# Attention scores of a MoBA and mLSTM block: three 64-row products per pair of heads, or two 128-row products per head with the split ahead of device memory

## The reference, cut to what matters

```python
h = rms_norm(x, pre_norm_g[l])
proj = jnp.einsum('bsd,dc->bsc', h, w_in[l])
aq, ak, av, az, mq, mk, mv, mo, mz, mi, mf = split_columns(proj)
ya = moba_attention(partial_rope(att_heads(aq), pos), partial_rope(att_heads(ak), pos), att_heads(av))
ya = rms_norm(ya, attn_out_g[l]) * jax.nn.silu(az)
...
s_own = jnp.einsum('hqd,hld->hql', q_c, k_own).astype(jnp.float32)
p = jax.nn.softmax(jnp.concatenate([s_sel, s_own], axis=-1), axis=-1)
...
y = jnp.einsum('bsc,cd->bsd', jnp.concatenate([ya, ym], axis=-1), w_out[l])
x = x + rms_norm(y, post_norm_g[l])
```

## Time and profile before

| what | value |
|---|---|
| median of 3 runs | 317.83 us (317.74 to 318.38) |
| the profiled execution | 317.99 us, its span 316.2 us |
| PE busy | 309.4 us, 98% of the span, granted clock 0.998 |
| DVE busy | 225.4 us, 71% |
| ACT busy | 165.2 us, 52% |
| POOL busy | 95.9 us, 30% |
| DMA | 38.30 MB, mean 121 GB/s |
| score products (L1758) | 96 of 64 rows by 128 |

### The profile page before, as it was taken

How to read it: one execution, slowest core, us unless ns; L and a number is a source line. 1 busy time by engine, 2 the same in 40 slices (tenths; PEclk the granted TensorE clock), 3 DMA queues, 4 the chain that set the end, 5 groups by cost and what they waited for, 6 DMA issues and landing times.

```text
span 316.2 us, 4992 instructions
## 1 busy us (share of the span) xinstructions
PE 309.4 (98%) x1599; PEld 256.4 (81%) x1599; DVE 225.4 (71%) x508; ACT 165.2 (52%) x336; POOL 95.9 (30%) x118
## 2 busy tenths in 40 slices
PE   8999999999999999999999999999999999999992
PEld 4888888888888888888888888778888888888882
DVE  2544999748998699968998568964577766856534
ACT  3548857287345324663157563384556876353301
POOL 8201006056350213002320025592711984000000
PEclk9999999999999999999999999999999999999999
DMA  7941553956725486645864332210220473310111
GB/s 222 323 99 38 153 149 93 170 163 150 134 68 146 134 158 205 188 124 122 180 227 151 102 90 77 73 66 31 67 68 0 125 200 145 133 68 0 68 66 67
DMA packets 29081, 38.30 MB, mean 121 GB/s; under 512 B 3624, under 2 KB 15184, under 8 KB 29056
## 3 DMA queue, kind: packets, MB, share of 16 engines
q1 hardware_dynamic: 27424, 34.51, 36.2%
q0 software_dynamic: 1472, 3.34, 7.0%
q10 hardware_dynamic: 160, 0.14, 0.1%
HBM read 33.68 MB, written 4.29 MB: 120 GB/s over the span
## 4 chain that ended last, share of the span: by engine, by line
PE 93%; issue 3%; DMA 2%; DVE 0%; DVEq 0%; SPq 0%; ACT 0%; POOLq 0%; POOL 0%; ACTq 0%
PE bank L1476 24%; PE bank L1478 24%; PE bank L1477 24%; PE bank L1814 3%; PE bank L1524 3%; PE bank L1758 3%; PE bank L1779 3%; PE bank L1612 2%; DMA farena<-in_x 2%; PE bank L1708 1%; PE bank L1505 1%; PE bank L1769 1%; PE bank L1613 1%; PE bank L1552 1%; PE bank L1551 1%
## 5 line engine op out<-in xcount | busy, mean ns | idle before, releaser
L778 ACT ACTIVATE w_hi<-w_raw 128x512 fp32r<-128x512 f32 x71 | 43.7, 626 | 63.2 <-PE bank L1478 51.1
L1476 PE MATMUL bank<-w_hi,xT_hi 128*128 128x512 f32 (+1 forms) x180 | 72.5, 403 | 0.0
L1478 PE MATMUL bank<-w_hi,xT_lo 128*128 128x512 f32 (+1 forms) x180 | 69.8, 388 | 0.0
L1477 PE MATMUL bank<-w_lo,xT_hi 128*128 128x512 f32 (+1 forms) x180 | 69.3, 385 | 0.0
L1043 DVE TENSOR_TENSOR w_lo<-w_raw,w_hi 128x512 fp32r<-128x512 f32 x64 | 45.5, 721 | 11.1 <-ACT w_hi L778 11.0
L1476 PE MATMUL bank<-xT_hi,w_hi 128*128 128x512 f32 x128 | 50.8, 397 | 0.0
L1478 PE MATMUL bank<-xT_hi,w_lo 128*128 128x512 f32 x128 | 50.1, 392 | 0.0
L1477 PE MATMUL bank<-xT_lo,w_hi 128*128 128x512 f32 x128 | 50.0, 390 | 0.0
L1478 PEld LDWEIGHTS bank<-w_hi,xT_lo 128*128 128x128 f32 x180 | 33.8, 188 | 7.2
L1476 PEld LDWEIGHTS bank<-w_hi,xT_hi 128*128 128x128 f32 x180 | 33.9, 188 | 5.8 <-issue 0.4
L1477 PEld LDWEIGHTS bank<-w_lo,xT_hi 128*128 128x128 f32 x180 | 34.0, 189 | 5.5
(11 more groups left out here) (211 smaller groups left out, 581.8 us busy)
## 6 DMA issues: line engine op xcount, KB each, us to landing
w_raw<-in_w_in SPq DMA_DIRECT2D x72, 256.0 KB, 2.9
w_raw<-in_w_out SPq DMA_DIRECT2D x16, 256.0 KB, 2.7
kq_rows<-stage SPq DMA_DIRECT2D x8, 256.0 KB
gy<-kq_rows SPq DMA_DIRECT2D x8, 256.0 KB, 3.5
gy<-in_x SPq DMA_DIRECT2D x4, 512.0 KB, 5.4
out_y<-gy SPq DMA_DIRECT2D x7, 256.0 KB, 2.1
farena<-in_x SPq DMA_DIRECT2D x4, 256.0 KB, 5.3
farena<-in_x SPq DMA_DIRECT2D x2, 512.0 KB, 7.5
```

Of the source, the lines that this page charges most:

```text
L778: a.activation(hi, raw, ACT.Copy).then_inc(w_hi_done, 1)
L1476: pe.matmul(o, hi, m_hi, start=start, stop=False)
L1477: pe.matmul(o, hi, m_lo, start=False, stop=False)
L1478: return pe.matmul(o, lo, m_hi, start=False, stop=stop)
```

## The change

The split into high and low parts moves ahead of device memory, where ACT writes the high part to `gate` and DVE the low part over `stage`. Each quarter is written out twice, high and low. What comes back is, for each head, one operand of 128 partitions: 64 high rows over 64 low rows (`keys`, `queries`), and for the queries a second one with the two halves exchanged (`swapped`). A head's scores are then two products of all 128 rows, stacked queries by stacked keys and exchanged queries by stacked keys, which adds the low-by-low product to the three. The reads move from SP to POOL: 8 for keys, 8 for queries, and 10 for the exchanged queries.

```diff
-OUT_AT, BACK_AT = (S_AQ + 6, S_AV + 6), (S_AQ + 8, S_AV + 8)
+HIGH_AT, LOW_AT = (S_AQ + 1, S_AV + 1), (S_AQ + 2, S_AV + 2)
+OUT_AT = (S_AQ + 13, S_AV + 13)
+FIRST_Q = 3
...
-OUT_CUTS = {0: 5, 1: 6, 2: 7, 3: 8, 12: 17, 13: 17, 14: 19, 15: 20}
+OUT_CUTS = {0: 5, 1: 8, 2: 9, 3: 11, 12: 17, 13: 17, 14: 19, 15: 20}
...
             def rows_out(w, m):
-                sp.wait_ge(kq_ready, NT * w + m + 1)
-                sp.dma_start(kq_dram[w, :, ROT * m:ROT * m + ROT, :], by_dims[:, m, :]).then_inc(kq_out[w], 16)
-            def rows_back(w, m):
-                sp.wait_ge(kq_out[w], 16 * NT)
...
+                for q, (done, src) in enumerate(((kq_hi, gate), (kq_lo, by_dims))):
+                    sp.wait_ge(done, NT * w + m + 1)
+                    sp.dma_start(kq_dram[w, :, q, ROT * m:ROT * m + ROT, :], src[:, m, :]).then_inc(kq_out[w], 16)
...
+                    if OUT_AT[w] <= n < OUT_AT[w] + NT:
+                        rows_out(w, n - OUT_AT[w])
...
+            def keys_back(h):
+                g.wait_ge(kq_out[0], 32 * NT)
+                g.dma_start(keys[:, h, :], head_rows(0, h).bitcast(F32R)).then_inc(keys_in, 16)
+            def queries_back(h):
+                g.wait_ge(kq_out[1], 32 * NT)
...
+                g.dma_start(queries[:, h, :], head_rows(1, h).bitcast(F32R)).then_inc(queries_in[h >= FIRST_Q], 16)
...
             for h in range(1, MH):
+                if h == MH - 1:
+                    for n in range(AH):
+                        keys_back(n)
                 decay_rows(h)
...
+            swapped_back(3)
+            for h in range(FIRST_Q):
+                queries_back(h)
             for b in range(S_MZ + 2, LAST_SLOT + 1):
                 cut(b + AHEAD)
...
                 if b == S_MZ + 5:
                     head_rsqrt(2 * MH - 1)
+                    for h in range(FIRST_Q, AH):
+                        queries_back(h)
+                    swapped_back(2)
...
-            def k_high(m):
-                a.wait_ge(kq_moved[0], 16 * NT)
-                a.activation(kT_hi[:, m, :], whole[:, m, :], ACT.Copy).then_inc(kt_hi, 1)
+            def kq_high(w, m):
+                a.wait_ge(kq_ready, NT * w + m + 1)
+                if w:
+                    a.wait_ge(kq_out[0], 32 * NT)
+                a.activation(by_dims_hi[:, m, :], by_dims[:, m, :], ACT.Copy).then_inc(kq_hi, 1)
             def v_copy(t):
                 projected(a, "av", t)
-                a.wait_ge(kq_out[1], 16 * NT)
+                a.wait_ge(kq_out[1], 32 * NT)
...
                 if w and m == 0:
-                    v.wait_ge(kq_out[0], 16 * NT)
+                    v.wait_ge(kq_out[0], 32 * NT)
...
+            def kq_low(w, m):
+                v.wait_ge(kq_hi, NT * w + m + 1)
+                v.tensor_tensor(by_dims_lo[:, m, :], by_dims[:, m, :], f32(by_dims_hi[:, m, :]),
+                                ALU.subtract).then_inc(kq_lo, 1)
...
+                pe.matmul(o, queries[:, h, t * P:(t + 1) * P], k, start=True, stop=False)
+                pe.matmul(o, swapped[t][:, h // 2, h % 2, :], k, start=False, stop=True).then_inc(score_ps, 1)
```

More of the change, by code:

```diff
@@ L115 @@
 N_WIDE = AH * (NT - 1)
-FOURS_FROM = AH * (NT - 2)
 EVENTS = {}
@@ L312, in build @@
         bcol = pcol[0:16, R_BIAS:R_END]
-        by_dims, whole = stage, gate
+        by_dims, by_dims_hi = stage, gate.bitcast(F32R)
+        by_dims_lo = stage[:].bitcast(F32R)
         rope_t = [f_part(F_COS, SEQ), f_part(F_SIN, SEQ)]
@@ L448, in build @@
         kq_out = [sem(f"kq_out{w}") for w in range(2)]
-        kq_moved = [sem(f"kq_moved{w}") for w in range(2)]
+        kq_hi = sem("kq_hi")
+        kq_lo = sem("kq_lo")
+        keys_in = sem("keys_in")
+        queries_in = [sem(f"queries_in{c}") for c in range(2)]
+        swapped_in = [sem(f"swapped_in{t}") for t in range(NT)]
         v_raw = sem("v_raw")
-        kt_hi = sem("kt_hi")
-        kt_lo = sem("kt_lo")
         v_hi_done = sem("v_hi_done")
         v_lo_done = sem("v_lo_done")
-        qt_hi = sem("qt_hi")
-        qt_lo = sem("qt_lo")
         score_ps = sem("score_ps")
@@ L872, in v_high @@
                              ACT.Copy).then_inc(v_hi_done, 1)
-            def q_high(m):
-                a.wait_ge(kq_moved[1], 16 * NT)
-                a.wait_ge(mpv_ps, MH * NT)
-                a.activation(q_hi[:, m, :], whole[:, m, :], ACT.Copy).then_inc(qt_hi, 1)
             def turn_high(n):
@@ L922, in _ @@
                             v_high(t)
-                if S_AQ + 5 <= b < S_AQ + 5 + NT:
-                    k_high(b - S_AQ - 5)
-                if S_MZ + 5 <= b < S_MZ + 7:
-                    q_high(2 * (b - S_MZ - 5))
-                    q_high(2 * (b - S_MZ - 5) + 1)
+                for w in range(2):
+                    if HIGH_AT[w] <= b < HIGH_AT[w] + NT:
+                        kq_high(w, b - HIGH_AT[w])
             def out_cut(n):
@@ L1290, in _ @@
                             v_low(m)
-                if S_AQ + 6 <= b < S_AQ + 6 + NT:
-                    k_low(b - S_AQ - 6)
+                for w in range(2):
+                    if LOW_AT[w] <= b < LOW_AT[w] + NT:
+                        kq_low(w, b - LOW_AT[w])
                 if b - 2 in PE_PV and PE_PV[b - 2][1] % 2 == 1:
@@ L1796, in _ @@
                 events = EVENTS.get(s, ())
[L1797 to L1801 removed]
+                if s < NU:
+                    scores(s)
                 for kind, what in events:
```

126 lines of the change are left out of this document (60 added, 66 removed).

## The result

| | before | changed |
|---|---|---|
| median, us | 318.14 (317.74 to 318.57, 6 runs) | 330.87 (329.64 to 332.75, 6 runs) |
| profiled execution, us | 317.99 | 330.92 |
| its span, us | 316.2 | 329.1 |
| PE's slot 56 begins, us | 182.51 | 192.61 |
| PE's last product begins, us | 310.36 | 322.76 |

The changed kernel takes 1.040 of the time before (95% interval 1.037 to 1.044). The forecast of 321.4 has the sign and less than a third of the size, and the time lies outside the range of 315.9 to 323.8.

What follows compares the result with a forecast made beforehand. PE was taken as the bound, with 93% of the chain of waits. From 317.99 us, -2.1 for PE's scores and +5.5 for the writes gave 321.4 us, range 315.9 to 323.8.

Steps and rivals of the forecast that it cites:

- The place and the sign: Release of `stage` to `v_copy`, just before PE's slot 56, decides; 321.4 us, 1.1% slower.
- Half of them work: DMA engines during writes: busy 0.48 of the time at 186 GB/s, so 256 KB takes 1.4 us.
- Term 2: Writes of keys and queries from `stage`: late release starts slot 56 near 188.0, not 182.5; +5.5 us, bounds nothing to 7.
- The stall of head 3: PE waits for DVE's `qk_low` of head 3 after slot 52: 0.6 us, inside the 5.5, no own term.
- rival 2: PE's clock falls in the 4.9 us stall before slot 56, losing 1.7 us: 323.1 us; chance 0.15.
- Term 1: PE's attention scores: two 128-row products per head take 9.7 us in place of 11.8; -2.1 us, bounds 2.1 and 0.3.
- The signs: Trace marks listed beforehand to show each step right or wrong, such as PE idle 4 to 5.5 us near 183.
- The edits costed at nothing: Splits, moved `q_high` and `q_low`, POOL's reads, later decay rows and mask waits: no time added.

Runs made afterwards that it cites:

- sixteen in the slowest dimension: Changed kernel with scratch rows reordered so each write's slowest dimension is 16, not 8; 322.68 us, ratio 1.014 to the kernel before.
- keys alone with sixteen: Changed kernel with only the keys' rows written and read with slowest dimension 16, queries keeping 8; 326.17 us, ratio 1.024 to the kernel before.
- reads on SP: Changed kernel with the four exchanged reads of the last tile on SP in place of POOL; 330.61 us, ratio 1.036 to the kernel before.
- one slot earlier: Changed kernel with each pair of writes one slot earlier in SP's order; 328.39 us, ratio 1.033 to the kernel before.
- PE kept at work: Changed kernel with 24 unread products of 512 columns into an idle bank ahead of slot 56; 329.00 us, ratio 1.035 to the kernel before.
- loads cut: Changed kernel with weight loads of slots 60 to 65 cut to 16 of 512 columns; 325.14 us, ratio 1.023 to the kernel before.

## Why the prediction was wrong, step by step

- **The place and the sign were right.** PE stood still just before slot 56, ended by `v_copy` (L907), which waited for the writes, and DVE was held near 147. "Half of them work" was right too: sixteen in the slowest dimension took 8 us off.
- **Term 2, the length of a burst, is the step that failed.** "Eight writes with three loads between them take 8 x 1.4 + 3 x 0.7 = 13.3 us", with 1.4 more to land, gave 14.7; the bursts lasted 17.0 and 16.6 us. The two prices were right (the write's came from a single stretch of 1 us in the earlier trace rows, which was lucky): 1.35 us a write with the loads' bytes away, and 11.5 to 12.0 us from the first landing to the last, where the sum had 11.9. What was too small is the start. The first write was to land 2.8 us after its issue and took 4.8 and 4.9. Some 0.9 of that went with the loads' bytes, so it belongs to the loads that already stood in front, which the sum took as none. The other 1.3 us stayed (4.1 in place of 2.8), and no run shows their cause.
- **The same error twice in a chain.** The keys came 17.0 us after 134.0, so DVE was held 3.8 us, not 1.6. The first write of the queries then went at 175.2, not 172.5. That is 2.7 us, and the longer second burst 1.9: together the 4.6 by which slot 56 missed its 188.0 (0.44 of it is the offset in which the two executions stood apart from the start). The stall of head 3 was 3.1 us, not 0.6, but lies inside the sum as the prediction said: without it (keys alone with sixteen) slot 56 waited 6.6 us in one piece.
- **The clock (rival 2) came on top, and wasn't weighed as it should have been.** It was given 0.15 beside a stall of 4.9 us. Its price was 2.65 us in the changed kernel's trace, not 1.7, because PE worked 5.7 us at the lower level, not 3 to 4. In three other traces with a stall of 5 us or more it was 1.6, 2.3 and 2.8, so it varies from one execution to the next and 1.7 lies among the values.
- **Term 1, -2.1 us, was -0.3.** The pieces: the score products cost 10.13 us where they were to cost 9.7 (0.21 a head at 128 keys in place of 0.17, 0.119 a product at 256 in place of 0.11), and 9.94 before. The operations behind them got 1.16 us shorter, not 1.8; the four transposes do last 0.44, without the 0.15. And the stall on `num` took 0.76 back. The chain in the attention of the changed kernel, to be read beside the earlier trace rows:

```profile
230.11 0.47 PE bank L1800 x4
230.58 0.23 PE bank L1781
230.81 0.23 PE bank L1782
231.05 0.44 PE bank L1832 x4
```

- **The end, 0.4 us, had no term.** POOL's 26 more transfers were costed by their issue alone.
- The sum with the measured sizes: 321.4 + 4.6 (bursts and offset) + 2.65 (clock) + 1.8 (term 1) + 0.4 (end) = 330.85, against 330.92. It is bookkeeping of two executions and has to come out; it tests nothing by itself.
- **The signs.** Held: the score pairs with starts 0.23 apart at 512 columns and no gap behind them, `v_copy` waiting for the writes, DVE waiting near 147. Not held: 16.6 us from SP's first query write to the release (14 to 15 forecast), a DMA share of 0.67 from 180 to 187 (0.5 forecast, as if no load moved beside the writes), 6.0 us of idle PE (4 to 5.5), and 0.6 us of idle PE inside the attention.
- **The edits costed at nothing** cost nothing: POOL's key reads (4.29 us for eight), the later decay rows and the reads ahead of the cut of slot 68 show no wait of PE in the changed kernel.

## What to carry to other kernels

Count a burst's length with everything that stands in its queue, what is there before the first transfer too, and take the first landing from a burst of the same kind, not from a lone store (4.8 us and 2.1 here). If the result releases a buffer that starts the next burst, the error counts twice. The writes whose slowest dimension was 8 used half of the engines; reordering the rows of the scratch tensor was worth 8 us here, though it doubled the exchanged reads, and these brought a stall of their own until they moved to SP. Of transfers moved to POOL, count also their number at the end of the program, and of a stall of some us, the clock behind it.

## What the runs showed that I had not expected

- POOL's closing drain grows by 0.082 us with each transfer that POOL issued (2.88 us for 27, 5.82 for 63), whatever its bytes.
- The lower clock didn't follow the length of a stall alone. At the scores of head 3 stalls of 3.1, 2.9 and 1.6 us left the clock up (changed kernel, reads on SP, one slot earlier), and stalls of 2.9 and 2.7 us in the same place brought it down (PE kept at work, loads cut). With sixteen one of 1.6 us at 269 was enough.
- One product on DVE with two inputs in SBUF takes 0.74 us where POOL isn't cutting. Beside POOL's cuts it took 1.38 to 1.59 us in fifteen traces, 4.08 us in one, and 0.73 us in the one where it stands a step later. The 4.08 us came with the one execution of 324.8 us.
- Two profiled executions of nearly the same program begin their first slots up to 2.7 us apart (8.44 and 11.14 us for the start of slot 0's last product), so a stage is compared by its own length, not by its place in the span.
